# The last back-projection of a stage and the first two products of the next, each half of the tokens through all its weight panels

## What is computed

```python
def sublayer_input(x, g, mod_j):
    shift, scale, gate = mod_j[:, 0], mod_j[:, 1], mod_j[:, 2]
    h = rmsnorm(x, g) * (1 + scale[:, None, :]) + shift[:, None, :]
    return h, (1 + gate)[:, None, :]
def swiglu(h, w_gu, w_down):
    g, u = jnp.split(h @ w_gu, 2, axis=-1)
    return (jax.nn.silu(g) * u) @ w_down
# per layer: x = x + 0.5 * g * swiglu(h); x = x + g * mixer(h); x = x + 0.5 * g * swiglu(h)
# first block ends in rmsnorm(x, final_norm_g); then twice (norm, hybrid), and rmsnorm again
def hybrid_layer(x, norm_g, w_in, w_br_a, w_br_b, w_br_c, w_out, cos, sin):
    h = rmsnorm_2(x, norm_g)
    proj = h @ w_in
    ...
    return x + merged @ w_out
```

## Time and profile before

| | us |
|---|---|
| median of 3 runs (lowest, highest) | 3655.68 (3654.98, 3667.2) |
| the profiled execution, its own time | 3663.32 |
| its span in the trace | 3661.6 |
| TensorE matmul busy | 3317.2 (91%) |
| ScalarE, VectorE, GpSimd busy | 1171.5, 1702.0, 610.5 |
| mean granted clock of TensorE | 0.943 |

### The profile page before, as it was taken

One profiled execution on the slowest core, in us unless ns is written; L12 is line 12 of the kernel. 1 busy time (PEld: TensorE's weight loads), 2 busy tenths in 40 slices (PEclk: granted clock), 3 DMA queues, 4 the chain that ended last, 5 costly groups with the idle time before them and its releaser, 6 DMA issues. The chain is left out here.

```text
span 3661.6 us, 37829 instructions
## 1 busy us (share of the span) xinstructions
PE 3317.2 (91%) x15684; PEld 2691.4 (74%) x15684; DVE 1702.0 (46%) x2451; ACT 1171.5 (32%) x1589; POOL 610.5 (17%) x331
## 2 busy tenths in 40 slices
PE   4999889998999899988789997888989988899898
PEld 4888775777888788876578886666767776567687
DVE  5555652236532533354443336585642248755313
ACT  3222234343222322234532223233452222334322
POOL 0000001011000000014310000323233323223242
PEclk7999999998999999999899998988999999889899
DMA  5555440313532223222122222312212222212131
GB/s 214 182 185 184 172 139 25 114 70 130 197 99 92 81 94 102 87 91 79 45 78 97 92 91 62 95 52 74 65 58 81 84 84 78 62 51 70 58 98 52
DMA packets 286548, 353.64 MB, mean 97 GB/s; under 512 B 9458, under 2 KB 263210, under 8 KB 286378
## 3 DMA queue, kind: packets, MB, share of 16 engines
q1 hardware_dynamic: 286378, 351.23, 29.3%
HBM read 336.00 MB, written 2.10 MB: 92 GB/s over the span
## 5 line engine op out<-in xcount | busy, mean ns | idle before, releaser
L498 PE MATMUL psum<-h_high,w_high 128*128 128x512 f32 x2624 | 1039.6, 396 | 45.8 <-POOL w_low L2123 17.6
L498 PE MATMUL psum<-h_low,w_high 128*128 128x512 f32 x2624 | 1032.0, 393 | 0.0
L498 PE MATMUL psum<-h_high,w_low 128*128 128x512 f32 x2624 | 1031.3, 393 | 0.0
L2123 POOL TENSOR_TENSOR w_low<-raw,w_high 128x2048 fp32r<-128x2048 f32 (+3 forms) x111 | 491.4, 4428 | 2419.6 <-ACT w_high L1005 2409.3
L1005 ACT CAST w_high<-raw 128x2048 fp32r<-128x2048 f32 (+2 forms) x254 | 467.5, 1841 | 725.0 <-PE psum L498 596.5
L498 PEld LDWEIGHTS psum<-h_high,w_high 128*128 128x128 f32 x2624 | 499.0, 190 | 160.7 <-issue 35.9
L498 PEld LDWEIGHTS psum<-h_high,w_low 128*128 128x128 f32 x2624 | 498.3, 190 | 106.7
L498 PEld LDWEIGHTS psum<-h_low,w_high 128*128 128x128 f32 x2624 | 499.2, 190 | 104.3 <-issue 0.5
L1494 DVE TENSOR_TENSOR w_low<-raw,w_high 128x2048 fp32r<-128x2048 f32 (+1 forms) x143 | 318.9, 2230 | 309.2 <-ACT w_high L1005 309.0
L498 PE MATMUL psum<-y_high,w_high 128*128 128x512 f32 x688 | 271.4, 394 | 26.5 <-DVE y_low L1638 16.8
L498 PE MATMUL psum<-y_low,w_high 128*128 128x512 f32 x688 | 269.5, 392 | 0.0
(11 more groups left out here) (256 smaller groups left out, 4388.1 us busy)
## 6 DMA issues: line engine op xcount, KB each, us to landing
raw<-in_ffn_w_gu SPq DMA_DIRECT2D x88, 1024.0 KB, 5.1
raw<-in_mod_w SPq DMA_DIRECT2D x72, 1024.0 KB, 5.5
raw<-in_w_in SPq DMA_DIRECT2D x64, 1024.0 KB, 5.1
raw<-in_ffn_w_down SPq DMA_DIRECT2D x32, 1024.0 KB, 5.1
raw<-in_ffn_w_down SPq DMA_DIRECT2D x16, 768.0 KB, 4.4
raw<-in_sb_w_qkv SPq DMA_DIRECT2D x12, 1024.0 KB, 5.2
area<-area SPq DMA_DIRECT2D x92, 128.0 KB, 2.4
raw<-in_lru_w_in SPq DMA_DIRECT2D x10, 1024.0 KB, 5.2
```

Of the source, the lines that this page charges most:

```text
L498: mm = e.matmul(psum[0:width, base + m, :], wv[a][:, at_k, c0:c0 + width], X[b][:, k, :], start=(at_k == 0 and (a, b) == (0, 0)), stop=(at ...
L2123: e.tensor_tensor(low[:, :n], raw[m % NRAW][:, :n], high[:, :n].bitcast(F32), ALU.subtract).then_inc(*q.up(s_plow, "w_low", x))
```

## The change

All eight ends of stages are rewritten.

- **Back-projection.** The last back-projection of each stage runs half 0 of the tokens through all four panels, then half 1 through all four (banks `BACK_BANK`). So each of its panels is loaded, cast and split twice: a panel is listed once per half (`half_panels`). The two column blocks are the outer loop and k the inner.
- **First products.** The first two products of the next stage (`FIRST`) run as first half 0, second half 0, first half 1, second half 1, with their panels loaded twice as well.
- **Who makes w_low.** Of the eight back panels VectorE takes the first six and GpSimd the last two; GpSimd takes all four of the first products.
- **Norm.** Squares go over two tiles at a time. All of half 0's squares come beside the first half, its spread and apply beside the second; half 1's norm beside the first products. `end1` and h0's norm are one pass, with two sums and two spreads.
- **Buffers.** Four `raw` buffers, and `w_low` is written over `raw` in place; three `w_high`. A raw buffer is free after the product. While mod_w panels come, these have the fourth buffer to themselves. Near halves, casts and splits run two panels ahead.
- sb's panels are reordered (q, k, q, k, v, v); in h0 and h1 the a_v product comes second, before i_k.

TensorE issues 960 more rows of matmuls, 14864 for 13904.

```diff
-        NRAW, NW = 3, 2
-        raw = [sb(f"raw{i}", [P, RAW]) for i in range(NRAW)]
-        W = [(sb(f"w_high{i}", [P, RAW], F32R), sb(f"w_low{i}", [P, RAW], F32R)) for i in range(NW)]
+
+        NRAW, NW = 4, 3
+        raw, w_low = [], []
+        for i in range(NRAW):
+            with nc.sbuf_tensor(f"raw{i}", [P, RAW], F32) as r:
+                raw.append(r)
+            w_low.append(sb(f"w_low{i}", [P, RAW], F32R))
+        w_high = [sb(f"w_high{i}", [P, RAW], F32R) for i in range(NW)]
...
+        SB_ORDER = ((0, 0), (1, 0), (0, 2), (1, 2), (2, 0), (2, 2))
+
+        FIRST = {"sb": ((0, 0, 0), (1, 0, 0)), "lru": (("gate", 0), ("x", 0)), "h0": (("i_q", 0), ("a_v", 0)), "h1": (("i_q", 0), ("a_v", 0))}
+        FIRST.update({stage: (("gate", 0), ("up", 0)) for stage in FFN})
+        FIRST_BANK, BACK_BANK, NORM_BANK = (2, 4), ((0, 1, 2, 3), (4, 5, 0, 1)), (6, 7)
...
+        def half_panels(stage, parts, by_vector=()):
+
+            for h in range(2):
+                for i, (what, pieces) in enumerate(parts):
+                    halves.add(len(panels))
+                    panel(stage, (*what, h), pieces, "DVE" if (i, h) in by_vector else "POOL")
+
+        def back_panels(stage, row0, w, nk, last=True):
+            parts = [(("back", row0, c), [piece(w[row0 * P:(row0 + nk) * P, c * PANEL:(c + 1) * PANEL], nk)]) for c in range(NC)]
+            if last:
+                half_panels(stage, parts, [(c, 0) for c in range(NC)] + [(0, 1), (1, 1)])
+                return
...
+                allowed = range(NRAW)
+            else:
+                allowed = [NRAW - 1] if kind == "mod" else range(NRAW - 1)
...
+            return ("mod_sum", i) if kind == "mod" else ("product", *panels[i][0])
+
+        def ahead_of(i):
+
+            return min(i + (2 if i + 1 in halves else 1), len(panels) - 1)
...
+            def first_products(stage):
+
+                for h in range(2):
+                    for p, what in enumerate(FIRST[stage]):
+                        key, base = (stage, *what), FIRST_BANK[p]
+                        base_of[key] = base
+                        i, w, total = w_views(*key, h)
+                        take(i)
+                        if h == 0:
+                            wait_free(base)
+                            wait_free(base + 1)
+                        wv = [x[:, :total].rearrange("p (k n) -> p k n", n=PANEL) for x in w]
+                        wait_panel(i)
+                        tokens = what == ("a_v", 0)
+                        for at_ in range(2 * KD):
+                            k = at_ % KD if tokens else at_ // 2
+                            for step in h_ready(stage)(k, h):
+                                q.wait_ge(*at(*step))
...
+                                if tokens:
+                                    tt = 2 * h + at_ // KD
+                                    mm = e.matmul(psum[:, base + h, (tt % 2) * PANEL:(tt % 2) * PANEL + PANEL], H[b][:, k, tt * P:(tt + 1) * P], wv[a][:, k, :],
+                                                  start=first, stop=last)
+                                else:
+                                    m = at_ % 2
+                                    mm = e.matmul(psum[:, base + m, HALF[h]], wv[a][:, k, m * P:(m + 1) * P], H[b][:, k, HALF[h]], start=first, stop=last)
+                            if h == 0 and stage != "f0":
+                                if (p, at_) == (0, 11):
+                                    gather(stage, 1)
+                                if (p, at_) == (1, 11 if stage == "h0" else 3):
+                                    broadcast(stage, 1)
...
+                for h in range(2):
+                    for c in range(NC):
+                        key, bank = (stage, "back", row0, c, h), BACK_BANK[h][c]
+                        i, w, total = w_views(*key)
+                        take(i)
+                        wait_free(bank)
+                        wv = [x[:, :total].rearrange("p (k n) -> p k n", n=PANEL) for x in w]
+                        wait_panel(i)
+                        for m in range(2):
+                            for at_k, k in enumerate(ks):
+                                for hh in range(2):
+                                    for step in x_ready(k, hh):
+                                        q.wait_ge(*at(*step))
+                                for a, b in COMBOS:
+                                    mm = e.matmul(psum[:, bank, m * S // 2:(m + 1) * S // 2], wv[a][:, at_k, m * P:(m + 1) * P], X[b][:, k, HALF[h]],
+                                                  start=(at_k == 0 and (a, b) == (0, 0)), stop=(at_k == nk - 1 and (a, b) == COMBOS[-1]))
+                            if m == 1:
+                                mm.then_inc(*q.up(s_product, "product", *key))
+                            if h and (c, m) == (0, 1):
+                                gather(to_norm, 0)
+                            if h and (c, m) == ((2, 0) if to_norm == "h0" else (1, 1)):
+                                broadcast(to_norm, 0)
...
+                    take((stage, *first, 0))
+                else:
+                    take((stage, *first, 0))
+                    apply(stage, 0, 5)
+                take((stage, *second, 0))
+                if stage != "f0":
+                    spread(stage, 1)
+                apply(stage, 1)
+                take((stage, *first, 1))
+                take((stage, *second, 1))
...
+                for c in range(NC):
+                    take((stage, "back", row0, c, 0))
+                    squares(to_norm, c, 0)
+                for c in range(NC):
+                    take((stage, "back", row0, c, 1))
+                    squares(to_norm, c, 1)
+                    if c == 0:
+                        spread(to_norm, 0)
+                    if c in (1, 2):
+                        apply(to_norm, 0, (0, 0, 2)[c], (0, 2, 5)[c])
...
+                for c in range(NC):
+                    add(c, 0)
+                    if c:
+                        squares(to_norm, c - 1, 0)
+                squares(to_norm, NC - 1, 0)
+                add(0, 1)
                 spread(to_norm, 0)
-                split_after((stage, "back", row0, whole + 1))
-                add(0, 1)
-                squares(to_norm, 1, 0, 2 * whole + 2)
                 add(1, 1)
-                begin(to_norm, 2 * whole + 2)
+                apply(to_norm, 0, 0, 2)
+                squares(to_norm, 1, 1)
+                add(2, 1)
+                apply(to_norm, 0, 2, 5)
+                squares(to_norm, 2, 1)
+                add(3, 1)
+                squares(to_norm, 3, 1)
```

732 lines of the change are left out of this document (345 added, 387 removed).

## The result

The changed kernel takes 3723.2 us, the kernel before 3657.6 us (medians of four runs each): 1.0173 times as long, 95% interval 1.0155 to 1.0191. It is slower, as forecast, and inside the range; of the 66 us between the medians the forecast (39) had somewhat over half.

The account below looks back on a forecast made before the run. The prediction took the chain add, squares, spread, apply on VectorE and ScalarE at the steps as the bound. It summed 14 + 13 + 13 - 7 + 6 = 39 on 3655.7 to 3695 us; own range 3672 to 3728, 8-in-10 range 3590 to 3735.

Parts of the forecast that it names:

- halving: On TensorE, 960 matmuls of 512 columns cut in two, 0.24 for 0.227 us, nothing hiding it: +14 us.
- starts of the last back-projections: TensorE waits for the last two y_low, 2.5 us at four feed-forward ends (+10), and lru +3: +13 us.
- losses of the steps: Seven steps between stages: time beyond TensorE's work there, lost to held VectorE instructions and slow clock, 164.5 against 152: +13 us.
- h0 and h1: TensorE's 6.3 us wait for a_v's w_low becomes 1.9 us for a_q's, less some for the rope chain: -7 us.
- f0's start: Both halves are spread before the first product, with three GpSimd splits beside it: +5 us, bounds 0 and 12.
- end: At the kernel's end, apply of k 5 to 7 comes ahead of half 1's spread: +1 us.
- half 0's norm inside the back-projection: No term of its own; only 0.9 us for gather and broadcast in lru's start.
- the load term: Steps f0 to sb and sb to f1: the fourth panel's load waits for the first product, +5.4 us each.
- (a): Rival: in the steps GpSimd's splits miss the chain, VectorE slips between, no fall of the clock: 3578 us; chance 0.24.
- (b): Rival: one of each step's two waits, the spread's or k 5's, falls away, 46 us: 3649 us; chance 0.19.
- (c): Rival: SyncE's order in the mod stages has no slack, 36 pairs by 2 us: 3767 us; chance 0.07.
- the sign that would have made the forecast wrong altogether: TensorE waiting inside the stages for w_high or w_low, that is for raw buffers; no size given.

Follow-up runs that it names:

- e5: The changed kernel, with raw buffers taken in turn for all loads instead of one for mod panels and three for weight panels: 3716.4 us, 1.0139 of the kernel before.
- e1: The changed kernel, with w_low of every half panel except f0's first products split by VectorE instead of GpSimd: 3689.9 us, 1.0078 of the kernel before.
- e6: The changed kernel, with k 0 to 3 of the third column block begun before k 4 of the first in last back-projections: 3741.2 us, 1.0211 of before.
- e9: The changed kernel, with TensorE's gather and broadcast for half 0's norm later in the feed-forward stages' last back-projections: 3729.4 us, 1.0188 of before.
- e10: The changed kernel, first products' panels prepared once, the second split late by VectorE, raw buffers in turn, lru's decay behind sb's first products: 3594.0 us, 0.9815 of before.
- e2: The changed kernel, with half 1's root (ScalarE) and spread (VectorE) ahead of the fourth half panel's cast and take: 3682.9 us, 1.0060 of the kernel before.

## Why the prediction was right, and where it was not

Direction, the mechanism of the steps and the range held: the splits meet the chain in all seven steps, in the adds of squares ahead of k 5 and in the spread's products. The forecast itself was 27 us short, mainly because one term was missing. Term by term, on the 59.5 us of the profiled executions:

| term | predicted | measured |
|---|---|---|
| halving | +14 | 960 x 0.013, pitch 0.12 as before: +13 |
| starts of the last back-projections | +13 | waits of 1.2, 2.0, 2.3 and 2.3 us in f0 to f3, nothing in lru: +8 |
| losses of the steps | +13 | 170.6 - 151.6 = +19 |
| h0 and h1 | -7 | -12, without their halving -14; unsettled, see below |
| f0's start | +5 | about +2 |
| end | +1 | 16.7 for 16.9 from the last back product: 0 |
| half 0's norm inside the back-projection | none | waits of 19 us: +19, and slow matmuls |

The measured ones come to 47; some 10 of the other 12 are the slow matmuls told below.

**The steps.** For lru to f3 the prediction laid out waits of 6.7 and 6.8 us and a length of 40.4; 8.07, 6.11 and 42.50 were measured. It had both splits in their places; the second one holds the second add of squares (L1615), where the prediction had h_low of k 5. The two steps that needed a load were forecast at 28 and 23 and came to 33.4 and 26.9: there the load term was 5.4 for 8 us, as e5 shows, and at f0 to sb the decay for lru, 4.5 us of tiny instructions on VectorE, also moved from behind apply of half 0 to ahead of its k 5 to 7. f3 to h0 came out under its 34.

**The step that failed** is what lies between the starts and the steps. The prediction gave gather and broadcast of half 0 their 0.9 us in lru and nothing in the other stages, and let nothing wait for them. TensorE's instructions run in the order of its program, and it meets these two in the middle of the half-1 back products while VectorE has not finished half 0. TensorE's rows in after, for f0, f1, f2 and f3:

```profile
438.85 0.58 PE L578 MATMUL psum<-ones,area 128*128 128x1 f32 x4 [2.69 <-DVE area L1615]
1248.87 0.70 PE L586 MATMUL psum<-inv,ones 128*128 128x256 f32 x2 [2.79 <-DVE inv L1645]
1641.23 0.70 PE L586 MATMUL psum<-inv,ones 128*128 128x256 f32 x2 [2.59 <-DVE inv L1645]
2289.43 1.87 PE L578 MATMUL psum<-ones,area 128*128 128x1 f32 x8 [7.91 <-DVE area L1615]
```

With 1.34 in f0, 1.03 in sb and 0.85 in f2 these are 19.2 us. In the back-projections of f0, f1, f2 and f3, 19 to 34 matmuls of 256 columns each start every 0.21 instead of 0.12 us, behind these waits and those of the start: another 1.7 to 3.1 us each, 10.5 in all.

In f0, f1 and f2 the diagonal is late by the very mechanism that the prediction knew from the steps. GpSimd splits the last two back panels in a row, and both products of half 0's spread fall beside them. In after, f1, and then the second product in e1, where VectorE splits:

```profile
1241.17 6.92 POOL L2186 TENSOR_TENSOR w_low<-raw,w_high 128x1536 fp32r<-128x1536 f32 x2 [362.20 <-ACT w_high L1073]
1243.29 1.41 DVE L1636 TENSOR_TENSOR small<-small 128x2 f32<-128x2 f32 x1
1244.74 3.37 DVE L1638 SCALAR_TENSOR_TENSOR small<-small 128x2 f32<-128x2 f32 x1
```

```profile
1240.82 0.16 DVE L1638 SCALAR_TENSOR_TENSOR small<-small 128x2 f32<-128x2 f32 x1
```

In e1 the three waits for the diagonal and the 0.85 in f2 are gone, and of the 7.91 us in f3, where an add of squares was held for 3.64 us, 3.39 are left. The other 3.7 us, at the gathers in f0 and sb, stay (2.76 and 0.99), so these are not the holding; what makes them isn't shown. In lru nothing waits, and that was the only stage the sum looked at. This was luck: the spread came between the two splits with under 1 us to spare, and in e6 it no longer does. e9 shows that moving the two instructions in TensorE's order doesn't bring the time back.

**h0 and h1.** Whether there is a gain is unsettled, and the reason was wrong. TensorE was to wait 1.9 us for a_q's w_low and waits 6.40:

```profile
2373.75 0.77 PE L541 MATMUL psum<-h_high,w_high 128*128 128x512 f32 x1 [6.40 <-POOL w_low L2186]
```

ScalarE makes two copies of 1.0 us ahead of that cast, not one, and a GpSimd instruction of 1.78 us for the rope stands ahead of its split. The wait has changed its name, from a_v to a_q. The 12 us themselves are one profile's: the stretch from the step to h0 to the next one is 646.3 us in after and 656.2 in e9 with the same instructions, and over h0 and h1 together the gain on before is 12 us in after, 7 in e9 and 1 in e5. What makes them differ stays open.

**The starts.** The waits in f2 and f3 are 0.92 and 1.38, as worked out (0.9 and 1.6); in f0 and f1 TensorE waits once, for 1.15 and 2.00 us, and in lru the waits are 10.5 and 10.7 us where one of 16.26 stood, but the stretch between its two steps is no longer than before: 213.8 us and the 10.9 of the second product, now in the step, for 225.2. **The rivals.** (a) needed VectorE to slip between the splits; in no step of after does it. e10 comes within 16 us of (a)'s 3578, but by other means (two splits and two loads fewer per stage), so that is no support for (a). (b) was one of the two waits falling away: that is e2, and its price was right, 46 us forecast and 45 measured; it ended 20.6 us over the kernel before, since (b), too, had nothing for half 0's norm. (c) asked for waits inside the stages with mod_w, and behind f0's first products there are none for a panel. In lru, h0 and h1 TensorE does wait for w_low inside the stages, 1.1 to 6.6 us at a time, but it did so before (1.0 to 6.6), so the sign that would have made the forecast wrong altogether did not appear. **A slip in the sum.** In lru's start the 30 matmuls left of the first half-panel are put at 5.4 us; at 0.12 they are 3.6.

## What to carry to other kernels

Count what a finer order loads, casts and splits again, and look at which engine and in which stretch: here the second set of first panels cost 104 us, and all the rest of the change gained 38. Before an instruction is put into an in-order queue, ask what the engine behind it will wait for there: a cast that waits for a product, ahead of a 0.2 us root, was 45 us. A wait that can be shortened isn't a gain until the next consumer in the chain has been looked at (e6, e9).
